# State-space outputs summed in one PSUM bank, and the gate taken from that bank

## The reference, cut to what matters

```python
# _ssd_scan, one chunk, per direction
cb = jnp.einsum('btgn,bsgn->btsg', ci, bi)
y = jnp.einsum('btsg,btsge,bsgep->btgep', cb, Lm, xi)                          # inside the chunk
y = y + jnp.einsum('btgn,bgenp->btgep', ci, S) * jnp.exp(cum)[..., None]       # from the carried state
# _mixer
o_b = scan_forward + flip(scan_backward)
o_b = o_b + lp['d_skip'].reshape(SSM_GROUPS, SSM_HPG, 1) * xh                  # skip
o_b = o_b.reshape(Bn, L, SSM_INNER) * jax.nn.silu(z)                           # gate
o_b = rms_norm_3(o_b.reshape(..., SSM_GROUPS, 512), lp['ssm_norm_w'])          # norm over a group
y_b = o_b @ lp['w_pb']
```

## Time and profile before

| | us |
|---|---|
| median of the runs | 3501.8 |
| the profiled execution's own time | 3501.87 |
| its span, first to last instruction | 3500.1 |
| PE busy | 3251.3 |
| DVE busy | 2113.5 |
| ACT busy | 1250.0 |
| POOL busy | 1370.7 |

### The profile page before, as it was taken

How to read it: one execution, slowest core, us unless ns; L and a number is a source line. 1 busy time by engine, 2 the same in 40 slices (tenths; PEclk the granted TensorE clock), 3 DMA queues, 4 the chain that set the end, 5 groups by cost and what they waited for, 6 DMA issues and landing times. The chain is left out here.

```text
span 3500.1 us, 44694 instructions
## 1 busy us (share of the span) xinstructions
PE 3251.3 (93%) x17806; PEld 2617.4 (75%) x17806; DVE 2113.5 (60%) x2504; ACT 1250.0 (36%) x1899; POOL 1370.7 (39%) x625
## 2 busy tenths in 40 slices
PE   8999998999989898999999989898999868899998
PEld 6778777888866677977888867667886646678886
DVE  6586865889855476354756544968983787631112
ACT  4333343323244332233423342334441655332222
POOL 3434343444332234434344433326641322334443
PEclk9999999999999999999999999998999989999999
DMA  3223353464333245444444322533233765422322
GB/s 120 91 91 127 118 185 125 160 243 164 119 124 97 79 139 152 125 172 151 144 147 148 96 92 92 173 99 124 100 118 115 211 175 151 154 82 86 104 93 76
DMA packets 237662, 451.26 MB, mean 129 GB/s; under 512 B 59936, under 2 KB 120032, under 8 KB 230416
## 3 DMA queue, kind: packets, MB, share of 16 engines
q1 hardware_dynamic: 230384, 437.93, 38.3%
q10 hardware_dynamic: 7072, 10.49, 0.8%
HBM read 396.88 MB, written 51.46 MB: 128 GB/s over the span
## 5 line engine op out<-in xcount | busy, mean ns | idle before, releaser
L288 POOL TENSOR_TENSOR third_feed_lo<-third_feed_raw,third_feed_hi 128x1024 fp32r<-128x1024 f32 (+3 forms) x191 | 449.2, 2354 | 834.3 <-ACT third_feed_hi L281 825.5
L288 POOL TENSOR_TENSOR second_feed_lo<-second_feed_raw,second_feed_hi 128x1024 fp32r<-128x1024 f32 (+3 forms) x182 | 407.4, 2241 | 638.4 <-ACT second_feed_hi L281 602.6
L288 POOL TENSOR_TENSOR first_feed_lo<-first_feed_raw,first_feed_hi 128x1024 fp32r<-128x1024 f32 (+4 forms) x182 | 396.3, 2181 | 552.8 <-ACT first_feed_hi L281 543.3
L186 PE MATMUL shared_ps<-third_h_hi,third_feed_hi 128*128 128x512 f32 (+1 forms) x776 | 322.4, 415 | 39.9 <-ACT third_in_rows_bend L794 18.7
L187 PE MATMUL shared_ps<-third_h_lo,third_feed_hi 128*128 128x512 f32 (+1 forms) x776 | 310.7, 400 | 0.0
L188 PE MATMUL shared_ps<-third_h_hi,third_feed_lo 128*128 128x512 f32 (+1 forms) x776 | 310.6, 400 | 0.0
L281 ACT ACTIVATE third_feed_hi<-third_feed_raw 128x1024 fp32r<-128x1024 f32 (+3 forms) x191 | 190.9, 1001 | 294.1 <-PE shared_ps L188 79.5
L281 ACT ACTIVATE second_feed_hi<-second_feed_raw 128x1024 fp32r<-128x1024 f32 (+3 forms) x182 | 173.8, 956 | 198.8 <-PE ffn_low L188 70.7
L281 ACT ACTIVATE first_feed_hi<-first_feed_raw 128x1024 fp32r<-128x1024 f32 (+4 forms) x182 | 168.6, 929 | 209.6 <-PE mixer_acc L188 79.8
L186 PE MATMUL mixer_acc<-first_h_hi,first_feed_hi 128*128 128x512 f32 x544 | 221.3, 407 | 8.4 <-DVE first_h_lo L1406 6.3
L480 DVE SCALAR_TENSOR_TENSOR ffn_ada_sum<-ffn_ada_w,cond,ffn_ada_sum 128x512 f32<-128x512 f32 x196 | 217.2, 1124 | 4.0
(11 more groups left out here) (783 smaller groups left out, 7989.4 us busy)
## 6 DMA issues: line engine op xcount, KB each, us to landing
third_feed_raw<-in_stream SPq DMA_DIRECT2D x156, 512.0 KB, 3.5
second_feed_raw<-in_stream SPq DMA_DIRECT2D x130, 512.0 KB, 3.5
first_feed_raw<-in_stream SPq DMA_DIRECT2D x120, 512.0 KB, 3.3
ffn_ada_w<-in_w_ada SPq DMA_DIRECT2D x48, 1024.0 KB, 5.3
scratch_gates<-mixer_gate ACTq DMA_DIRECT2D x32, 256.0 KB, 2.1
mix_gin<-scratch_gates SPq DMA_DIRECT2D x32, 256.0 KB, 3.3
x_res<-scratch_cum SPq DMA_DIRECT2D x16, 512.0 KB, 7.1
shared_seg<-scratch_cum SPq DMA_DIRECT2D x16, 512.0 KB, 7.5
```

Source lines behind the costliest of these rows:

```text
L186: nc.tensor.matmul(out, w_hi, x_hi, start=start, stop=False)
L288: eng.tensor_tensor(self.lo[:, p % self.cut, :n], self.raw[:, p % self.deep, :n], self.hi[:, p % self.cut, :n].bitcast(F32), ALU.subtract) ...
```

## The change

In part 1, chunk `c` now begins with four skip matmuls into bank 6 + c % 2 (L4094 of the changed kernel): a diagonal matrix with `d_skip` on it, times the x tile. The 16 inside matmuls accumulate on it, and the two decayed inter products, which VectorE still makes in `y` and `tmp`, are added to the same bank by two matmuls with the identity (`add_inter`, L4107 and L4109). VectorE then takes the gate straight from the bank (L4266), one instruction for each chunk. VectorE's two additions (L4301, L4304) and the skip instruction (L4238) are gone. ScalarE makes the four diagonals of each group in `core.pick` (`skips`, 128 x 128 each). The inter product of chunk c+1 is issued before `add_inter` of chunk c. The loads of `xg` and `z` are cut by chunk instead of by channel tile, so a partition's row is four pieces of 512 bytes instead of one of 2 KB. Those of chunks 2 and 3 are issued within part 1, ahead of `load_e(g, 5)` and `load_e(g, 7)`, and no longer at the start of the next group (for group 3 no longer after part 1).

```diff
+                def load_gate(g, c):
+                    n = 4 * g + c
                     if n >= 2:
                         sp.wait_ge(gated, n - 1)
+                    for to, at in ((xg, dram["xbc"][T * g:T * (g + 1)]),
+                                   (z, dram["z"][Z3["z"] + T * g:Z3["z"] + T * (g + 1)])):
+                        sp.dma_start(to[:, c % 2], rows(at)[:, :, c * P:(c + 1) * P]).then_inc(xz_in[c % 2], 16)
...
                     for n in range(2 if g < 3 else 0):
                         load_cum(g + 1, n)
+                    load_gate(g, 2)
                     load_e(g, 5)
...
                     load_e(g, 6)
+                    load_gate(g, 3)
                     for n in range(2, 4 if g < 3 else 0):
                         load_cum(g + 1, n)
                     load_e(g, 7)
...
+                def intra(g, c):
+                    bank = ps[:, 6 + c % 2]
+                    n = 4 * g + c
+                    if c == 0:
+                        pe.wait_ge(skip_made, 4 * g + 4)
+                    else:
+                        pe.wait_ge(gated, n - 1)
+                    pe.wait_ge(xz_in[c % 2], 32 * (n // 2 + 1))
+                    for j in range(4):
+                        nc.tensor.matmul(bank[:, j * P:(j + 1) * P], skip[:, j], xg[:, c % 2, j], start=j == 0,
+                                         stop=False, skip_group_check=True)
...
+                def add_inter(g, c):
+                    pe.wait_ge(read, 8 * g + 2 * c + 2)
+                    nc.tensor.matmul(ps[:, 6 + c % 2], core.ident[:], y[:, :, c * P:(c + 1) * P], start=False,
+                                     stop=False, skip_group_check=True)
+                    nc.tensor.matmul(ps[:, 6 + c % 2], core.ident[:], tmp[:], start=False, stop=True,
+                                     skip_group_check=True).then_inc(y_summed, 1)
...
+                    inter(g, 0)
                     for c in range(4):
...
+                        intra(g, c)
+                        if c < 3:
+                            inter(g, c + 1)
+                        add_inter(g, c)
                         fill(g, 1, c)
...
+                def skips(g):
+                    if g:
+                        act.wait_ge(y_summed, 4 * g)
+                    for j in range(4):
+                        a.activation(skip[:, j], core.ident[:], ACT.Copy, scale=core.v("d_skip", 4 * g + j)
+                                     ).then_inc(skip_made, 1)
...
-                def gate(g, some):
-                    for j in some:
-                        n = 4 * g + j
-                        dve.wait_ge(y_made, 4 * g + 4)
-                        dve.wait_ge(xz_in[j % 2], 32 * (n // 2 + 1))
-                        v.scalar_tensor_tensor(out=y[:, j], in0=xg[:, j % 2], scalar=core.v("d_skip", n), in1=y[:, j],
-                                               op0=ALU.mult, op1=ALU.add).then_inc(skipped, 1)
-                        dve.wait_ge(skipped, n + 1)
-                        v.tensor_tensor(y[:, j], y[:, j], z[:, j % 2], ALU.mult).then_inc(gated, 1)
+                def gate(g, c):
+                    n = 4 * g + c
+                    dve.wait_ge(y_summed, n + 1)
+                    dve.wait_ge(xz_in[c % 2], 32 * (n // 2 + 1))
+                    v.tensor_tensor(y[:, :, c * P:(c + 1) * P], ps[:, 6 + c % 2].rearrange("p (j t) -> p j t", t=P),
+                                    z[:, c % 2], ALU.mult).then_inc(gated, 1)
...
-                    dve.wait_ge(read, 8 * g + 2 * c + 2)
-                    v.tensor_tensor(part, part, by_channel(tmp[:]), ALU.add).then_inc(added, 1)
-                    dve.wait_ge(added, 4 * g + c + 1)
-                    dve.wait_ge(intra_ready, 8 * g + 2 * c + 2)
-                    v.tensor_tensor(part, part, by_channel(ps[:, 6 + c % 2]), ALU.add).then_inc(y_made, 1)
...
-                    if g:
-                        gate(g - 1, (0, 1))
...
-                    if g:
-                        gate(g - 1, (2, 3))
...
                     for c in range(4):
                         if c < 3:
                             mask(g, c + 1)
+                        if c:
+                            gate(g, c - 1)
                         out(g, c)
                         dense.vector(dve, before(g, 1) if c == 0 else pieces_by(g, 1, c - 1))
+                    gate(g, 3)
```

81 lines of the change are left out of this document (35 added, 46 removed).

## The result

| | before | changed |
|---|---|---|
| median of the runs, us | 3501.92 (4 runs) | 3523.4 (4 runs, 3520.87 to 3532.9) |
| ratio | | 1.0069 [1.0054, 1.0084] |
| profiled execution's own time | 3501.87 | 3532.9 |
| its span | 3500.1 | 3531.1 |

What follows compares the result with a forecast made beforehand. TensorE was taken as the bound in part 1 of groups 0 and 2, VectorE in group 1, part 1, and group 2, part 0. 15.1 - 3.8 + 1.0 - 2.0 + 4.3 + 1.9 = 16.5 gave 3518 us, range 3503 to 3537.

Steps and rivals of the forecast that it cites:

- group 0, part 1: Skip and inside product wait for late z, 4.3, plus 10.8 of added matmuls: +15, between 10 and 20.
- group 1, part 0: Without the gates ahead of it on VectorE, eviction L3878 comes 2.8 earlier, and 1 from a shorter slow start: -3.8.
- group 1, part 1, to the first state product of group 2: Up to L4221, TensorE's lateness lies mostly under VectorE's old work, 5.6 of it gate instructions now gone: +1, between -5 and +6.
- rest of group 2, part 0 (clock): TensorE, with 18.26 us busy at 0.67 of its clock, starts less cold: -2.
- group 2, part 1, and group 3, part 0: Matmuls 10.8, less the 1.94 wait for L3878 and 1.8 for the clock; gate gone in group 3, -2.8: +4.3.
- group 3, part 1: With the tail: z lands late, skip starts at 2991, but the gate is one instruction: +1.9, between -4 and +7.
- the signs that were named: What the later profile should show, including no idle before L4148 in group 3 and ScalarE's gate waits before L4161 gone.
- The turned wait: Group 1, part 1: add_inter waits for VectorE's products until 2848.4, tiles queued behind it; idle before L4107 4 us or more.
- the rival of VectorE's relief: VectorE's path decides in groups 1 and 2; -12 in all, 3490; sign: first add_inter of group 1 waits under 1 us; chance 0.12.
- TensorE starts less cold: Rest of group 2, part 0: TensorE, before at 0.67 of its clock, loses less to slow starts: -2.
- That of the clock: Rival: added matmuls close idle stretches in group 1, part 1, and group 2, part 0, clock stays up: -11, 3507; chance 0.13.
- That of the transfers: Rival: gate inputs in 512-byte pieces land late in a full queue, 3.4 more for each group's first: +19, 3537; chance 0.12.

Runs made afterwards that it cites:

- before_plus_matmuls: The kernel before, with the change's six f32 matmuls per chunk added on TensorE ahead of the inside product, results unused; 3520.84 us, 1.0052 of before.
- before_less_vector: The kernel before without VectorE's two additions L4301 and L4304 and skip L4238, output lacking these terms; 3486.85 us, 0.9963 of before.
- early_inputs: The changed kernel with the gate inputs of chunks 0 and 1 of each group loaded at the start of part 0; 3517.74 us, 1.0043 of before.
- decays_first: Against a kernel with ScalarE scaling the skip, VectorE adding, and early inter products: gate loads of chunks 2 and 3 put behind the decay loads; 3495.38 us, 0.9989 of before.
- before_inter_first: The kernel before, with only TensorE's inter product of chunk c+1 issued before the projection tiles of chunk c; 3492.95 us, 0.9992 of before.
- early_tiles_first: The changed kernel with early gate inputs, and the slot's projection tiles before the two identity products; 3519.78 us, 1.0064 of before.

## Why the prediction was right, and which of its terms were not

| term | forecast | by the parts of the trace |
|---|---|---|
| group 0, part 1 (part 0: -0.8) | +15.1 | +15.5 |
| group 1, part 0 | -3.8 | -2.5 |
| group 1, part 1, to the first state product of group 2 | +1.0 | +2.5 |
| rest of group 2, part 0 (clock) | -2.0 | +0.6 |
| group 2, part 1, and group 3, part 0 | +4.3 | +7.2 - 3.6 |
| group 3, part 1 | +1.9 | +3.6 |

The sum was 16.5 and the stage gave 22.4. The mechanism was the forecast one: the matmuls go onto TensorE where it is the bound, the relief counts in part, and late inputs stop group 0. before_plus_matmuls and before_less_vector show the first two by themselves. The sum itself is 5.9 short, and none of that is in group 0. The whole kernel's +21.5 agrees with the stage, but its interval is 5 us to either side, so only the parts of the stage can test the terms.

Of the signs that were named, most came: L4107 and L4109 0.86 us each, L4094 0.245 apart, TensorE +45.4 and VectorE -33.9 us, 10.03 us of idling before L4094 in group 0, parts 1 of groups 0 and 2 longer by 15.5 and 7.2. Three did not. The idle before L4107 in group 1 was 0.81 us and not 4 or more; before L4148 in group 3 TensorE still idled for 0.68 and 1.64 us (2.78 before); and ScalarE still waited 25.1 us for the gate in the stage, half of the 49.8 of the kernel before.

*Group 0.* Right in size, with parts that offset: the idle was 10.03 us, not 8.5, since `z` was issued at 2767.64 - 6.84 = 2760.8 and took 5.0 to land, so that the skip started 0.85 later than taken, and the inter product ended 0.7 earlier (2762.76 - 6.84 = 2755.9); the slow start cost 4.5 us for the 20 matmuls, not 5.4. early_inputs returns 5.1 where 4.3 had been put on the wait.

*Group 1, part 0.* The eviction came 2.6 us earlier (idle 4.67 in the earlier trace rows, 2.10 now) but the 1 us for a shorter slow start didn't come.

*Group 1, part 1.* The turned wait was named, and wrongly placed. TensorE's and VectorE's rows:

```profile
2859.24 2.05 PE L4094 MATMUL shared_ps<-ssm_xg,pick 128*128 128x128 f32 x8 [7.05 <-DMA ssm_z<-scratch_z]
...
2867.69 1.13 PE L4107 MATMUL shared_ps<-ssm_y,ident 128*128 128x512 f32 x2 [0.81 <-DVE sumsq L4324]
```

```profile
2855.16 10.14 DVE L4259 TENSOR_TENSOR third_h_lo<-ssm_y,third_h_hi 128x512 fp32r<-128x512 f32 x4 [5.51 <-ACT third_h_hi L4202]
2865.22 1.21 DVE L4303 TENSOR_TENSOR x_res<-x_res,ssm_cb 128x1024 f32<-128x1024 f32 x1
...
2866.96 0.68 DVE L4324 TENSOR_TENSOR sumsq<-shared_ps,shared_spare 128x512 f32<-128x512 f32 x1
```

TensorE was stopped 7.05 us by the inputs, so only 0.81 of "4 us or more" was left at L4107; the low parts set the time in either case, as early_inputs shows with its 9.96. (The idle under 1 us there was the sign named for the rival of VectorE's relief; it came, but only because the wait for `z` stood in front.) What makes the low parts late is GpSimd, which the sum doesn't consider here. Four of them take 2.49 us in group 2 of the kernel before (from 2903.38), where POOL is idle, and 10.14 here:

```profile
2859.20 5.55 POOL L4034 TENSOR_TENSOR shared_seg<-shared_seg,ssm_cb 128x1024 f32<-128x1024 f32 x2
```

The four end at 2857.04, 2859.79, 2862.55 and 2865.30, each 0.55 us behind an instruction of POOL (2856.49, 2859.24, 2862.00 and 2864.75), and the kernel before has the same 0.55 four times. No run moves POOL's masks away from them, so what that would give back isn't shown. VectorE came to the weighted inputs at 2900.81, which, less the 6.84 and the 12.2 of the parts ahead, is +0.7 where +1 was forecast. Then this step of the sum failed: the weighted inputs were taken at their old 0.68 us each, and ScalarE's diagonals, which hold POOL up, were costed "at nothing" (1.2 us were allowed for that only on the way to the gate loads). The rows of ScalarE, POOL and VectorE at the start of group 2:

```profile
2895.57 1.27 ACT L4182 ACTIVATE pick<-ident,vec 128x128 f32<-128x128 f32 x4
```

```profile
2900.34 2.36 POOL L4034 TENSOR_TENSOR x_res<-x_res,ssm_cb 128x1024 f32<-128x1024 f32 x1 [1.98 <-ACT x_res L4176]
```

```profile
2900.81 2.43 DVE L4250 TENSOR_TENSOR ssm_xw<-ssm_xdt,ssm_w 128x512 f32<-128x512 f32 x1
```

The decay of the next mask came 1.27 us later on ScalarE, POOL's instruction began at 2900.34 instead of being over, and VectorE's, which reads SBUF alone, ended only 0.5 us after POOL's: 2.43 us instead of 0.68. In the kernel before POOL was done at 2877.8, as the next row shows, and three such instructions took 1.89 from 2881.07; here they took 3.63. That is the 1.8 between +0.7 and +2.5. An estimate from these rows: without the diagonals POOL would have been done at some 2901.5 and VectorE's instruction at 2902.0 instead of 2903.24, so they account for some 1.2 of the 1.8. The rest comes with VectorE's being early, now that no gate stands ahead: it comes to L4250 7.3 us after the group's first chunk product instead of 18.5. POOL in the kernel before:

```profile
2873.11 4.67 POOL L4036 TENSOR_TENSOR x_res<-x_res,ssm_cb 128x1024 f32<-128x1024 f32 x2 [27.61 <-DVE ssm_cb L4322]
```

The five kernels with the gate still in part 0 have 1.88 or 1.89 for the three. The others have 2.13 to 3.66, and the diagonals aren't needed for it: decays_first has none, and 3.65. POOL and VectorE there:

```profile
2877.05 2.35 POOL L4035 TENSOR_TENSOR x_res<-x_res,ssm_cb 128x1024 f32<-128x1024 f32 x1 [2.16 <-ACT x_res L4163]
```

```profile
2877.50 3.65 DVE L4239 TENSOR_TENSOR ssm_xw<-ssm_xdt,ssm_w 128x512 f32<-128x512 f32 x3
```

The prediction set a rule of the Trainium skill (SBUF — State Buffer, "Who interferes with whom") against rows, by which a VectorE instruction with two SBUF inputs contends with a GpSimd instruction that reads SBUF. These instructions and the four low parts agree with it, to the change's cost instead of its gain.

*The rest of group 2, part 0.* "TensorE starts less cold", -2, did not happen: the granted clock was 0.70, little above the 0.67 of before, and the first two state products (four records) took 3.78 us, as in the kernel before. TensorE idled 4.20 us ahead of them:

```profile
2903.30 3.78 PE L4148 MATMUL shared_ps<-ssm_xw,ssm_b_tok 128*128 128x512 f32 x4 [4.20 <-DVE ssm_xw L4250]
```

*Group 2, part 1.* +7.1 forecast, +7.2 measured, and before_inter_first shows its two relieving terms by themselves: 1.94 and 1.8 were taken, 3.75 measured. *Group 3.* The wait for `z` ended 0.9 us later than taken, half of the 1.7 that were missing (6.11 us of idling, the inputs issued behind four weight loads of 7.70 us):

```profile
3003.66 7.70 SPq L272 DMA_DIRECT2D third_feed_raw<-in_stream  x4
```

```profile
3017.53 2.04 PE L4094 MATMUL shared_ps<-ssm_xg,pick 128*128 128x128 f32 x8 [6.11 <-DMA ssm_z<-scratch_z]
```

Of the rivals, that of VectorE's relief had -12 for the stage with TensorE's price paid; before_less_vector has -12.6 without that price, so it was far off. That of the clock had 11 us come back in group 1, part 1, and group 2, part 0; the granted clock there was 0.82 and 0.70, against 0.81 and 0.67 before, so it stayed as it was. That of the transfers had the 512-byte pieces landing 3.4 us late; they landed in 5.0 to 5.9 us (4.7 to 5.7 before), so the pieces cost at most 0.3 each time and the place in the queue the rest.

The 17.7 us of order and waits are settled in part. 6.3 are the late inputs; that the place of the identity products costs anything isn't shown (early_tiles_first). The remaining 11.4, and the 4.8 that the earlier inter product should have given beside it, are not taken apart by a run, and their cause stays open; what the rows show for them is that the identity products can't fall into the waits for POOL and VectorE, as the matmuls of before_plus_matmuls do, since they come behind these waits (early_inputs: 4.43 and 9.96 us).

## What to carry to other kernels

An addition moved from VectorE to TensorE by an identity product can pay only where VectorE sets the end, and no run here shows a place where it did; price both engines part by part, and ask for the wait that the moved step brings, because work that can be issued early fills waits, and work that needs another engine's result of the same step does not. An input that becomes TensorE's instead of VectorE's has to be moved forward in the queue with it. And before moving work, try moving order: in one trace, one product issued ahead of the tiles was worth 4.8 us of the stage, more than any exchange here, though the runs of the whole kernel don't tell it from nothing. And look what the other engines do at the time: VectorE's latest instructions here were late because GpSimd ran beside them.

## What was not expected

- A wait of 1.94 us on TensorE took 3.7: the 1.7 behind it are projection tiles at a granted clock of 0.54, though TensorE had been busy throughout until the wait, at 1.00 just ahead of it. Elsewhere the same wait of 3.10 us was followed by 1.00 in one kernel and 0.55 in another, 2.9 us apart.
- f32 identity products of 128 x 512 are 0.86 us apart, against 0.23 for the fp32r tiles of the same size (L186 to L187).
- A VectorE instruction with SBUF operands took 2.43 us instead of 0.68 beside one of GpSimd, ending 0.54 behind it, and in nine kernels the first weighted input of group 2 ended 0.54 or 0.55 us behind GpSimd's mask. The four low parts of group 1 took 10 us instead of 2.5 in the same way.
